# A hybrid decoder step on one core: both token groups through the trunk together, or one after the other in plain fp32

## The chip, the cores and the metric

The kernel runs on one core of one Trainium2 chip. A core has a matrix engine (TensorE, called PE in the profile; PEld is its loading of weights), a vector engine (VectorE, DVE), an activation engine (ScalarE, ACT), a general engine (GpSimd, POOL), a sequencer for transfers (SyncE, SP) and 16 DMA engines that all queues share. The metric is device time of one execution in microseconds (us); lower is better. A bank is one of the eight accumulators of TensorE, of 512 fp32 numbers per partition.

## What is computed

Two groups of tokens share every parameter: a prompt of 512 tokens and a sample batch of 8 sequences by 4 tokens. Everything is fp32.

```python
xn = rmsnorm(x, g_mix)                                # D_MODEL = 2048
xr, yr, ca, cb, ga, gb = split(xn @ w_in)             # 1024, 1024, 1024, 1024, 2048, 2048 columns
xc = causal_dwconv(xr, width 4)
h  = rglru(xc)                                        # gates from 8 heads of 128x128, linear recurrence over time
branch_a = (h * gelu(yr)) @ w_a
dc = causal_dwconv(ca * sigmoid(cb), width 31)
branch_b = silu(layernorm(dc)) @ w_b
x  = x + (sigmoid(ga) * branch_a + sigmoid(gb) * branch_b) @ w_out
q  = rmsnorm(x, g_ffn) @ w_q                          # 8 heads of 2 x 128
s1, s2 = q1 @ keys1.T, q2 @ keys2.T                   # 128 keys each
e, sv = top-16 of the 256 sums of top16(s1), top16(s2)    # 16 of 16384 experts, per token and head
x  = x + sum_k softmax(sv)_k * gelu(u_tab[e_k] . xn) * v_tab[e_k]
y  = rmsnorm(x, g_final)
```

The convolution and recurrence states are inputs and outputs too. The expert step reads 128 rows of u_tab and 128 of v_tab (8 KB each) for every tile of 128 tokens, per head and per k.

## The kernel before

The tokens stand in five tiles of 128. **Group A** is one prompt tile and the 32 sample tokens (160 columns wide), **group B** the other three prompt tiles (384 columns). T = 544 is both.

- **Start.** Tokens are loaded, normalised and turned by TensorE into channels by tokens, 16 steps of five transposes (L1522, L1523), then split for the next loop into a rounded part `xh` and a rest `xl` (L738 on ACT, L1098 on DVE).
- **Channel loop**, 8 chunks of 128 channels, both groups at once (`product3`, L1571 to L1573). Each chunk makes four products (xr, yr, ca, cb) over 16 k-steps. The operands are split, so a k-step is three reduced-precision terms (hi*hi, hi*lo, lo*hi) on two halves of 272 columns: 6 matmuls. ACT (L713) and DVE (L1188, three pairs of pieces per chunk) or POOL (L615) split the weights. Beside it DVE runs the short convolution (L1142, L1145), the recurrence (L1154 to L1171) and the 31-tap convolution (`long_conv`, L1199 to L1213).
- **Branch pairs** of group A, then its output projection, its norm, its query projection (`product_pair`, L1588, plain fp32: 96 matmuls per branch pair, 32 per step of output or query), with transposes back to tokens (L1706) and scores (L1715).
- The same of **group B**. In all this time DVE also does **group A's expert rows**: 160 key rows (`dot_row`, L1357: multiply a gathered u row by the token and add up) and 96 of the 160 value rows (`value_row`, L1366), with the routing (`route`, L1311 to L1344) of each unit of 16 rows.
- **Group B's rows**: 256 key rows (L1418) on DVE with 16 routings, beside group A's last 64 value rows on TensorE (L1766, a diagonal matrix times the row) and the building of dense expert weights (L1442, L1788).
- **Last**: v_tab is streamed whole through TensorE for two of B's tiles (L1818), while the third tile has 128 key rows and 128 value rows of its own on DVE. The change does not touch this part.

Orders are written by hand: each engine executes its list in order and waits on semaphores. On DVE and ACT the numbers p of A's 160 steps are dealt out by `STEPS_Q`, `steps_branch`, `steps_out`, `STEPS_NORM`, `steps_query`: 14 beside A's query, 84 beside B's eight branch pairs, 20 beside its output, 3 beside its norm, 39 beside its query. `VALUE_AT` says after which key row a value row comes. POOL issues the gathers (L607): a key row may be fetched three ahead (`SLOTS_U`), a value row two ahead (`SLOTS_V`), so the gather of value row v waits until row v-2 has been added. Weights come by SP in pieces of 512 KB into four buffers; each is reused as soon as it has been multiplied. In the channel loop a piece is 128 columns wide (`piece`, packets of 512 bytes), elsewhere 256 (`columns`, 1 KB). All scores of group B are written to DRAM (L1036) before its second unit can be routed, since the routing reads them back (L934).

## Time and profile before

| what | us |
|---|---|
| median of three runs (3850.53 to 3858.8) | 3855.13 |
| the profiled execution | 3870.63 |
| its span, first to last instruction | 3868.8 |
| joint channel loop | 57.0 to 461.9 |
| group A's branches, output, query | 461.9 to 917.5 |
| group B's branch pairs | 917.5 to 1435.5 |
| its output and query | 1435.5 to 1857.7 |
| end of A's expert rows | 1905.6 |
| B's 256 key rows | 1912.4 to 2793.7 |

TensorE is busy 79% of the span, VectorE 67%, ACT 15%, POOL 36%; the transfers move 1244.91 MB at 322 GB/s on average. Read the shares by stage: before 460 the DMA engines are a third busy and TensorE is full; from 917 on they are nearly full, and VectorE is at seven to nine tenths. A plain fp32 matmul leaves two records in the trace, a reduced-precision one leaves one.

### The profile page before, as it was taken

The page shows a single profiled execution, that of the slowest core. Times are in us where ns is not written, and L with a number is a line of the kernel's source. Part 1 is how long each engine was busy: PE and PEld are TensorE (multiplying, and loading weights), DVE is VectorE, ACT ScalarE, POOL GpSimd, SP SyncE. Part 2 cuts the span into 40 slices and gives each one's busy share as a digit, 9 for nine tenths or more (in the row PEclk, how much of TensorE's full clock was granted, in tenths as well). Part 3 has the DMA queues.
Part 4 walks back from the last instruction along what each step waited for, and adds up shares of the span by engine and source line. Part 5 has one row for each costly group of instructions (what it writes and reads, how often), then busy time and mean ns, then how long its engine had stood idle before and what let it go on. Part 6 is the DMA issues. An engine that isn't in the chain of part 4 may idle for free.

```text
span 3868.8 us, 34526 instructions
## 1 busy us (share of the span) xinstructions
PE 3051.7 (79%) x11870; PEld 1937.8 (50%) x11870; DVE 2591.0 (67%) x3611; ACT 586.0 (15%) x1115; POOL 1394.5 (36%) x876
## 2 busy tenths in 40 slices
PE   6999989987999989888345544544179899999993
PEld 6999989975555545555112212222143334444441
DVE  2788830035777766666688887889985556665658
ACT  4444320010010000111100001222250000000000
POOL 2000000003343333324476667666612234434344
PEclk9999999989999999999676677777599999999996
DMA  4222367759899998889899999999849999999998
GB/s 125 85 84 85 97 188 241 238 191 353 327 383 391 369 380 333 321 339 355 339 410 405 407 401 404 357 383 378 316 182 350 365 408 418 421 421 421 421 422 357
DMA packets 394596, 1244.91 MB, mean 322 GB/s; under 512 B 22785, under 2 KB 268289, under 8 KB 268959
## 3 DMA queue, kind: packets, MB, share of 16 engines
q0 software_dynamic: 120720, 876.60, 56.4%
q1 hardware_dynamic: 258944, 356.03, 26.4%
q10 hardware_dynamic: 14815, 10.87, 0.9%
q8 instruction: 56, 0.92, 0.1%
q14 instruction: 61, 0.50, 0.0%
HBM read 1232.26 MB, written 12.00 MB: 322 GB/s over the span
## 4 chain that ended last, share of the span: by engine, by line
DMA 35%; PE 27%; DVE 20%; issue 10%; POOL 5%; ACT 1%; SPq 1%; DVEq 0%; POOLq 0%; ACTq 0%
DMA region<-in_v_tab_dram,region 26%; PE ps L1588 14%; DVE region L1418 6%; DMA region<-in_u_tab_dram,region 5%; POOL region L607 5%; DVE region L1366 4%; PE ps L1571 3%; PE ps L1573 3%; PE ps L1572 3%; DVE region L1357 1%; DMA region<-in_w_q_dram 1%; DMA region<-scores_kept 1%; DVE region L1315 1%; DVE region L1312 1%; DMA region<-in_w_in_dram 1%
## 5 line engine op out<-in xcount | busy, mean ns | idle before, releaser
L607 POOL DMA_INDIRECT region<-in_u_tab_dram,region x544 | 886.8, 1630 | 1488.5 <-DVE region L1357 578.8
L1588 PE MATMUL ps<-region,region 128*128 128x160 f32 (+1 forms) x5120 | 1208.7, 399 | 67.3 <-DMA region<-in_w_out_dram 20.1
L1588 PEld LDWEIGHTS ps<-region,region 128*128 128x128 f32 x5120 | 852.2, 194 | 415.5 <-issue 43.1
L1418 DVE SCALAR_TENSOR_TENSOR region<-region,region 128x2048 f32<-128x2048 f32 x384 | 869.5, 2287 | 105.0 <-DMA region<-in_u_tab_dram,region 104.3
L1818 PE MATMUL ps<-region,region 128*128 128x512 f32 x2048 | 890.4, 597 | 38.8 <-DMA region<-in_v_tab_dram 38.0
L1366 DVE SCALAR_TENSOR_TENSOR region<-region,region,region 128x2048 f32<-128x2048 f32 x224 | 526.8, 2352 | 560.5 <-DMA region<-in_v_tab_dram,region 548.9
L1818 PEld LDWEIGHTS ps<-region,region 128*128 128x128 f32 x2048 | 389.7, 191 | 538.9 <-issue 483.2
L607 POOL DMA_INDIRECT region<-in_v_tab_dram,region x288 | 469.5, 1630 | 423.8 <-DVE region L1366 338.6
L1766 PE MATMUL ps<-region,region 128*128 128x512 f32 x512 | 355.8, 861 | 330.3 <-DMA region<-in_v_tab_dram,region 305.7
L1766 PEld LDWEIGHTS ps<-region,region 128*128 128x128 f32 x512 | 139.2, 285 | 532.2 <-issue 505.9
L1357 DVE SCALAR_TENSOR_TENSOR region<-region,region 128x2048 f32<-128x2048 f32 x160 | 363.0, 2286 | 17.7 <-DMA region<-in_u_tab_dram,region 17.6
L1571 PE MATMUL ps<-region,region 128*128 128x272 f32 x1024 | 297.4, 290 | 0.0
L1573 PE MATMUL ps<-region,region 128*128 128x272 f32 x1024 | 296.4, 289 | 0.0
L1572 PE MATMUL ps<-region,region 128*128 128x272 f32 x1024 | 294.8, 288 | 0.0
L1788 PE MATMUL ps<-region,region 128*128 128x128 f32 x512 | 90.0, 336 | 198.5 <-DVE region L1442 179.8
L1572 PEld LDWEIGHTS ps<-region,region 128*128 128x128 f32 x1024 | 193.1, 189 | 0.0
L1571 PEld LDWEIGHTS ps<-region,region 128*128 128x128 f32 x1024 | 192.7, 188 | 0.0
L1573 PEld LDWEIGHTS ps<-region,region 128*128 128x128 f32 x1024 | 192.6, 188 | 0.0
L1788 PEld LDWEIGHTS ps<-region,region 128*128 128x128 f32 x512 | 80.5, 240 | 220.8 <-issue 215.6
L945 ACT ACTIVATE region<-region 128x16 f32<-128x16 f32 x34 | 7.4, 217 | 1212.8 <-DVE region L1418 916.1
L1205 DVE SCALAR_TENSOR_TENSOR region<-region,region,region 128x512 f32<-128x512 f32 (+1 forms) x232 | 156.8, 747 | 0.0
L625 POOL DMA_DIRECT2D region<-in_x_prompt_dram x1 | 0.6, 576 | 388.5 <-DVE region L1260 388.5
(227 smaller groups left out, 1681.0 us busy)
## 6 DMA issues: line engine op xcount, KB each, us to landing
region<-in_v_tab_dram SPq DMA_DIRECT2D x128, 1024.0 KB
region<-in_w_in_dram SPq DMA_DIRECT2D x192, 512.0 KB
region<-in_w_out_dram SPq DMA_DIRECT2D x64, 512.0 KB
region<-in_w_q_dram SPq DMA_DIRECT2D x64, 512.0 KB
region<-in_w_a_dram SPq DMA_DIRECT2D x32, 512.0 KB
region<-in_w_b_dram SPq DMA_DIRECT2D x32, 512.0 KB
region<-in_u_tab_dram,region POOLq DMA_INDIRECT x544, 12.0
region<-in_x_prompt_dram SPq DMA_DIRECT2D x7, 1024.0 KB, 16.1
```

The costliest lines, as they stand in the source:

```text
L607: pool.indirect_dma_start(out=slot, out_offset=None, in_=rows_ap, in_offset=bass.IndirectOffsetOnAxis(ap=idx[:, k:k + 1], axis=0)).then_in ...
L1205: mark(stt(out=run, in0=glupad[:, k:k + TP], scalar=tap(k), in1=run, op0=ALU.mult, op1=ALU.add))
L1357: stt(out=u_a[s], in0=u_a[s], scalar=1.0, in1=xn_tile(u), op0=ALU.mult, op1=ALU.mult, accum_out=dots[u % 2][:, p % TOPK:p % TOPK + 1]).the ...
L1366: stt(out=total, in0=v_a[s], scalar=w_all[:, e:e + 1], in1=total, op0=ALU.mult, op1=ALU.add).then_inc(v_added, 1)
L1418: stt(out=u_b[s], in0=u_b[s], scalar=1.0, in1=xn_tile(UNITS_A + u), op0=ALU.mult, op1=ALU.mult, accum_out=dots[u % 2][:, k:k + 1]).then_in ...
L1571: mm(halves[j][:, a, :], hi, xh[:, k, h], start=(k == 0), stop=False)
L1572: mm(halves[j][:, a, :], hi, xl[:, k, h], start=False, stop=False)
L1573: last = mm(halves[j][:, a, :], lo, xh[:, k, h], start=False, stop=(k == DC - 1))
L1588: last = mm(outs[n][:, 0:WIDTH[g]], wide[s][:, q, n * P:(n + 1) * P], rhs(k), start=(k == 0), stop=(k == n_k - 1))
L1766: last = mm(acc[0][:, b * 512:(b + 1) * 512], diag[:, m % ND, :], v_a[n % SLOTS_V][:, b * 512:(b + 1) * 512], start=first, stop=last_row)
L1788: last = mm(bank(4 + n % 4)[:, q * P:(q + 1) * P], one_b[n % 2][:, q, :], one_a[n % 2][:, q, :], start=True, stop=True)
L1818: last = mm(acc[n][:, b * 512:(b + 1) * 512], w, v_t[s][:, b * 512:(b + 1) * 512], start=(c == 0), stop=False)
```

## The change

The two groups go through the trunk one after the other, A first, each with its own channel loop, branches, output and query.

- The loop products are plain fp32 like all others (`product`: one matmul of 160 or 384 columns per k-step); the splitting of tokens and weights (`product3`, `high`, `low`, `xh`, `xl`) is gone. The part of w_in that the channel loop reads, 32 MB, is loaded twice.
- The start loads and turns A's two tiles only; B's tokens are turned (`first_channels(1)`) inside A's branches.
- The convolutions and the recurrence are called once per group and chunk, with 128 (plus sample) or 384 columns. B's read their left context from A's end, kept in `ex`.
- A's 160 expert steps are dealt out anew: 14 beside A's query as before, 48 beside B's channel loop, 64 beside its branch pairs, 17 beside output, 2 beside norm, 15 beside query.
- Value rows of A: 128 (was 96) on DVE among these steps, 32 (was 64) on TensorE among B's key rows; one addition of the accumulator instead of two.
- Prompt tile 0 is now in group A (it was tile 3), and the state rows go out in two halves from B's branches.

```diff
-ROWS_W = 6 * TOPK
+ROWS_W = 8 * TOPK
...
-GROUP_P = 2 * TOPK
...
+USE_C = (0, USES_CC + USES_G)
+USE_G = (USES_CC, 2 * USES_CC + USES_G)
...
-def steps_branch(m):
-    return 14 + 21 * m // 2, 14 + 21 * (m + 1) // 2
+STEPS_1, STEPS_2, STEPS_3, STEPS_4 = 14, 62, 126, 143
+STEPS_NORM = (STEPS_4, STEPS_4 + 2)
+
+
+def steps_chunk(c):
+    return STEPS_1 + (STEPS_2 - STEPS_1) * c // CC, STEPS_1 + (STEPS_2 - STEPS_1) * (c + 1) // CC
+
+
+def steps_branch(i):
+    return STEPS_2 + (STEPS_3 - STEPS_2) * i // PAIRS, STEPS_2 + (STEPS_3 - STEPS_2) * (i + 1) // PAIRS
 
 def steps_out(j):
-    return 98 + 2 * min(j, 10), 98 + 2 * min(j + 1, 10)
+    return STEPS_3 + (STEPS_4 - STEPS_3) * j // DC, STEPS_3 + (STEPS_4 - STEPS_3) * (j + 1) // DC
 
 def steps_query(h):
-    return 121 + 39 * h // HEADS, 121 + 39 * (h + 1) // HEADS
+    first = STEPS_NORM[1]
+    return first + (ROWS_A - first) * h // HEADS, first + (ROWS_A - first) * (h + 1) // HEADS
...
-            with sp.Fori(0, CC) as c:
-                block_of(0, w_in_v, c * P, (half_used[0], c * 2 + 1), (ca_done, c + 1))
-                block_of(1, w_in_v, c * P + CH, (half_used[1], c * 2 + 1), (cb_done, c + 1))
-                sp.wait_ge(igate_done, c + 1)
+            def block_of(pair, w, col, frees0, frees1):
+
+                piece(PAIR[pair][0], w, 0, col, *frees0)
+                piece(PAIR[pair][1], w, 1, col, *frees1)
+
+
+            def chunk_first(g, c, freed=((), (), (), ())):
+                half, done = c * 2 + (2 * CC * g + 1), c + (CC * g + 1)
+                block_of(0, w_in_v, c * P, ((half_used[0], half), *freed[0]), ((ca_done, done), *freed[1]))
+                block_of(1, w_in_v, c * P + CH, ((half_used[1], half), *freed[2]), ((cb_done, done), *freed[3]))
+
+            def chunk_rest(g, c):
+                half, done = c * 2 + (2 * CC * g + 2), c + (CC * g + 2)
+                sp.wait_ge(igate_done, c + (CC * g + 1))
                 sp.dma_start(gw[:, 0, :], w_r_v[:, c, :]).then_inc(gw_landed, 16)
                 sp.dma_start(gw[:, 1, :], w_i_v[:, c, :]).then_inc(gw_landed, 16)
-                block_of(0, w_in_v, c * P + 2 * CH, (half_used[0], c * 2 + 2), (xr_done, c + 2))
-                block_of(1, w_in_v, c * P + 3 * CH, (half_used[1], c * 2 + 2), (yr_done, c + 2))
-            sp.wait_ge(ca_done, CC + 1)
-            sp.wait_ge(cb_done, CC + 1)
+                block_of(0, w_in_v, c * P + 2 * CH, ((half_used[0], half),), ((xr_done, done),))
+                block_of(1, w_in_v, c * P + 3 * CH, ((half_used[1], half),), ((yr_done, done),))
+
+            def chunk_weights(g, between, freed=((), (), (), ())):
+                chunk_first(g, 0, freed)
+                between()
+                chunk_rest(g, 0)
+                with sp.Fori(1, CC) as c:
+                    chunk_first(g, c)
+                    chunk_rest(g, c)
...
-            def low(slots, n):
-                for s in slots:
-                    pool.wait_ge(hi_ready[s], n + 1)
-                    nc.gpsimd.tensor_tensor(wlo[s], wraw[s], whi_f[s], ALU.subtract).then_inc(lo_ready[s], 1)
...
+            chunk_first(0)
+            chunk_rest(0)
+            for c in range(1, CC):
+                first, end = steps_chunk(c - 1)
+                mid = (first + end) // 2
+                expert_steps(first, mid)
+                chunk_first(c)
+                expert_steps(mid, end)
+                chunk_rest(c)
...
-            def low(pair, use):
-
-                for s in PAIR[pair]:
-                    dve.wait_ge(hi_ready[s], use + 1)
-                    tt(wlo[s], wraw[s], whi_f[s], ALU.subtract).then_inc(lo_ready[s], 1)
...
+                for j in range(2, CW):
+                    run = odd if j % 2 else even
                     step.before(2)
-                    mark(stt(out=run, in0=glupad[:, k:k + TP], scalar=tap(k), in1=run, op0=ALU.mult, op1=ALU.add))
-                    if k == 2:
+                    mark(stt(out=run, in0=k.glu[:, j:j + m], scalar=tap(j), in1=run, op0=ALU.mult, op1=ALU.add))
...
+            short_conv(1, 0)
+            recurrence_and_unit(1, 0)
+            for c in range(1, CC):
+                first, end = steps_chunk(c - 1)
+                mid = (first + end) // 2
+                expert_steps(first, mid)
+                short_conv(1, c)
+                long_conv(1, c - 1)
+                expert_steps(mid, end)
+                recurrence_and_unit(1, c)
+            long_conv(1, CC - 1)
+            expert_steps(*steps_chunk(CC - 1))
+            norm_center(1)
+            norm_scale(1)
...
-            def add_group(n):
-                dve.wait_ge(v_used, (GROUP_P, ROWS_P)[n])
-                dve.wait_ge(v_added, ROWS_W)
-                tt(xf[n], xf[n], acc[0], ALU.add).then_inc(acc_read, 1)
+            def add_group():
+                dve.wait_ge(v_used, ROWS_P)
+                tt(xf[1], xf[1], acc[0], ALU.add).then_inc(acc_read, 1)
...
+            def first_channels(g):
+                pe.wait_ge(xn_ready, TILES[g].stop)
+                back = 4 - g
                 for k in range(DC):
-                    if k >= 4:
-                        pe.wait_ge(xT_dve, k - 3)
-                    if k == 2:
-                        pe.wait_ge(staged_read, 1)
-                    for t in range(NT - 1):
-                        tr(ps[:, k % 4, t * P:(t + 1) * P], xt[:, t, k * P:(k + 1) * P], ident)
-                    tr(ps[:, k % 4, TP:T], xt[0:TS, NT - 1, k * P:(k + 1) * P],
-                       ident[0:TS, 0:TS]).then_inc(xT_done, 1)
-                pe.wait_ge(xT_act, DC)
-                pe.wait_ge(xT_dve, DC)
+                    if k >= back:
+                        pe.wait_ge(xT_dve if (k - back) % 2 else xT_act, CC * g + (k - back) // 2 + 1)
+                    out = first_bank(g, k)
+                    for n, t in enumerate(range(TILES[g].start, TILES[g].stop)):
+                        q = TS if t == 1 else P
+                        last = tr(out[:, n * P:n * P + q], xtn[t][0:q, k * P:(k + 1) * P], ident[0:q, 0:q])
+                    last.then_inc(xT_done, 1)
...
-            def product3(j, pair, n, ready=None):
+            pe.wait_ge(staged_read, 3)
+
+            def product(out, pair, use, g):
                 for half, s in enumerate(PAIR[pair]):
-                    pe.wait_ge(lo_ready[s], n + 1)
+                    pe.wait_ge(w_landed[s], use * 16 + 16)
                     for q in range(KP):
                         k = half * KP + q
-                        if ready is not None:
-                            pe.wait_ge(ready, k + 1)
-                        hi, lo = whi[s][:, q * P:(q + 1) * P], wlo[s][:, q * P:(q + 1) * P]
-                        for a in range(2):
-                            h = slice(a * TH, (a + 1) * TH)
-                            mm(halves[j][:, a, :], hi, xh[:, k, h], start=(k == 0), stop=False)
-                            mm(halves[j][:, a, :], hi, xl[:, k, h], start=False, stop=False)
-                            last = mm(halves[j][:, a, :], lo, xh[:, k, h], start=False, stop=(k == DC - 1))
+                        last = mm(out[:, 0:WIDTH[g]], wraw[s][:, q * P:(q + 1) * P], xp[g][:, k, :],
+                                  start=(k == 0), stop=(k == DC - 1))
...
+            def chunk_products(g):
+                k, m, n0 = chunk[g], PROMPT[g], CC * g
+                with pe.Fori(0, CC) as c:
+                    pe.wait_ge(xr_padded, c + (n0 + 1))
+                    product(bank(0), 0, c * 2 + USE_C[g], g).then_inc(xr_done, 1)
+                    pe.wait_ge(yg_ready, c + (n0 + 1))
+                    product(bank(2), 1, c * 2 + USE_C[g], g).then_inc(yr_done, 1)
+                    pe.wait_ge(staged_read, 5)
+                    pe.wait_ge(glu_ready, c + (n0 + 1))
+                    product(bank(6), 0, c * 2 + (USE_C[g] + 1), g).then_inc(ca_done, 1)
+
+                    pe.wait_ge(gw_landed, c * 32 + (32 * n0 + 32))
+                    pe.wait_ge(xcv_ready, c + (n0 + 2))
+                    for s, (read, done) in enumerate(((rg_ready, rgate_done), (ig_ready, igate_done))):
+                        pe.wait_ge(read, c + (n0 + 1))
+                        last = mm(bank(1 + 2 * s)[:, 0:m], gw[:, s, :], k.xcv[:, 0:m], start=True, stop=True)
+                        if g == 0:
+                            last = mm(bs(bank(1 + 2 * s)[:, m:NA]), gw[:, s, :], xc_s, start=True, stop=True)
+                        last.then_inc(done, 1)
+                    pe.wait_ge(cg_ready, c + (n0 + 1))
+                    product(bank(7), 1, c * 2 + (USE_C[g] + 1), g).then_inc(cb_done, 1)
...
+            def branches(g):
+                done = CC * (g + 1)
+                pe.wait_ge(xr_padded, done + 1)
+                gate_a(g, 0)
+                pe.wait_ge(rg_ready, done + 1)
+                gate_b(g, 0)
+                pe.wait_ge(glu_ready, done + 1)
+                pe.wait_ge(dc_ready, done)
+                if g:
+                    for c in range(CC):
+                        last = tr(ps[0:E_N, 3, c * P:(c + 1) * P], ex[:, c, :], ident)
+                    last.then_inc(exT_done, 1)
+                pe.wait_ge(ig_ready, done + 1)
+                norm_mean(g)
+                pe.wait_ge(ha_ready, done + 1)
+                if g:
+                    pe.wait_ge(exT_read, 2)
+                    branch_a(g, 0)
+                pe.wait_ge(mean_read, g + 1)
+                norm_squares(g)
+                if g == 0:
+                    first_channels(1)
+                    branch_a(g, 0)
+                pe.wait_ge(sd_ready, g + 1)
+                branch_b(g, 0, ready=lambda k: (silu_ready, g * CC + k + 1))
+                with pe.Fori(1, PAIRS) as i:
+                    branch_pair(g, i)
+
+            branches(0)
...
             second_half(0)
-            pe.wait_ge(xp_ready, 5)
-            with pe.Fori(0, DC // 2) as i:
-                branch_pair(1, i)
+            chunk_products(1)
+            branches(1)
             second_half(1)
```

On TensorE, the first chunk of the channel loop. Before (region_49 and region_50 are the two parts of the tokens, region_51 and region_52 those of the weights):

```order
L1563 ISA
L1571 MATMUL ps<-region_49,region_52 128x272
L1572 MATMUL ps<-region_50,region_52 128x272
L1573 MATMUL ps<-region_49,region_51 128x272
L1571 MATMUL ps<-region_49,region_52 128x272
```

With the change, in A's loop (region_62 is A's tokens, 49 to 52 the four weight buffers as they land):

```order
L1599 MATMUL ps<-region_62,region_49 128x160 x8
L1599 MATMUL ps<-region_62,region_50 128x160 x8
L1599 MATMUL ps<-region_62,region_51 128x160 x8
L1599 MATMUL ps<-region_62,region_52 128x160 x8
L1596 ISA
L1599 MATMUL ps<-region_62,region_49 128x160 x8
```

Six matmuls of 272 columns per k-step became one of 160 here, and one of 384 later in B's loop.

On VectorE, inside the 31-tap convolution. Before, the splitting of weights (L1188) stands between taps:

```order
L1205 SCALAR_TENSOR_TENSOR region_114<-region_59,region_116,region_114 128x512
L1188 TENSOR_TENSOR region_51<-region_55,region_52 128x1024
L1188 TENSOR_TENSOR region_51<-region_56,region_52 128x1024
L169 REGISTER_ALU
L1205 ISA
L1205 SCALAR_TENSOR_TENSOR region_61<-region_59,region_116,region_61 128x512
```

With the change, the end of the convolution in B's loop; region_78 to region_80 hold gathered key rows, region_81 a value row:

```order
L1239 SCALAR_TENSOR_TENSOR region_68<-region_121,region_123,region_68 128x384
L1246 TENSOR_TENSOR region_68<-region_68,region_121 128x384
L1376 SCALAR_TENSOR_TENSOR region_80,region_116<-region_80,region_54 128x2048
L1368 RECIPROCAL region_116<-region_116 128x1
L1370 SCALAR_TENSOR_TENSOR region_123<-region_116 128x16
L1376 SCALAR_TENSOR_TENSOR region_78,region_116<-region_78,region_54 128x2048
L1385 SCALAR_TENSOR_TENSOR region_53<-region_81,region_123,region_53 128x2048
```

Expert rows now stand between the convolution and the recurrence of every chunk of B.

On POOL, the gathers among B's key rows. Before:

```order
L607 DMA region_78<-in_v_tab_dram,region_116 128x2048
L607 DMA region_90<-in_u_tab_dram,region_116 128x2048
L607 DMA region_82<-in_u_tab_dram,region_116 128x2048
L607 DMA region_83<-in_u_tab_dram,region_116 128x2048
L607 DMA region_79<-in_v_tab_dram,region_116 128x2048
```

With the change:

```order
L635 DMA region_92<-in_u_tab_dram,region_123 128x2048
L635 DMA region_93<-in_u_tab_dram,region_123 128x2048
L635 DMA region_82<-in_v_tab_dram,region_123 128x2048
L635 DMA region_85<-in_u_tab_dram,region_123 128x2048
L635 DMA region_86<-in_u_tab_dram,region_123 128x2048
L635 DMA region_94<-in_u_tab_dram,region_123 128x2048
L635 DMA region_87<-in_u_tab_dram,region_123 128x2048
```

A value row came every three or four key rows; it comes every seven now.

## Rows read from the trace of the kernel before

**Rows 1.** The page, the span in 40 slices of 96.7 us, busy tenths

```profile
DVE  2788830035777766666688887889985556665658
```

**Rows 2.** Timeline of PE: start us, us, line, count [idle before <-releaser]

```profile
23.50 1.25 PE L1511 MATMUL ps<-region,region 76*128 76x76 f32 x8 [23.50 <-DMA region<-in_state_rnn_h_dram]
...
51.08 3.44 PE L1550 MATMUL ps<-region,region 120*128 120x120 f32 x16 [1.67 <-ACT region L738]
...
56.98 0.37 PE L1571 MATMUL ps<-region,region 128*128 128x272 f32 x1
...
466.81 20.57 PE L1588 MATMUL ps<-region,region 128*128 128x160 f32 x128 [4.89 <-DVE region L1230]
...
917.47 34.12 PE L1588 MATMUL ps<-region,region 128*128 128x384 f32 x96 [4.19 <-DVE region L1305]
```

**Rows 3.** The chain that ended last, in time: start us, us, what, records

```profile
566.28 165.17 PE ps L1588 x1216
...
835.85 13.47 DMA region<-in_w_q_dram
...
1607.99 20.64 PE ps L1588 x64
```

**Rows 4.** Busy time by stretch: PE, PEld, DVE, ACT, POOL, clock, DMA share, GB/s

```profile
200.00:250.00 50.00, 50.00 (x390) 49.04 (x389) 41.66 (x68) 20.82 (x27) 0.00 (x0) 1.00 0.30 87
...
2000.00:2100.00 100.00, 48.66 (x64) 18.76 (x64) 82.97 (x129) 8.99 (x19) 67.61 (x39) 0.68 1.01 413
```

**Rows 5.** Timeline of DVE: scan, short and long convolution of one chunk

```profile
209.75 1.31 DVE L1166 TENSOR_TENSOR_SCAN region<-region 128x552 f32<-128x552 f32 x1
...
223.37 2.72 DVE L1145 SCALAR_TENSOR_TENSOR region<-region,region,region 128x568 f32<-128x568 f32 x3 [0.15 <-DVE region L1142]
...
240.22 8.70 DVE L1205 SCALAR_TENSOR_TENSOR region<-region,region,region 128x512 f32 x13
```

**Rows 6.** Timeline of DVE: the same operation at 160 and at 384 columns

```profile
495.23 1.98 DVE L1238 TENSOR_TENSOR region<-region,region 128x160 f32<-128x160 f32 x8
...
534.78 3.84 DVE L1238 TENSOR_TENSOR region<-region,region 128x384 f32<-128x384 f32 x8
```

**Rows 7.** Timeline of DVE: key rows (L1357) and a value row (L1366)

```profile
1115.76 2.29 DVE L1357 SCALAR_TENSOR_TENSOR region<-region,region 128x2048 f32<-128x2048 f32 x1
...
1117.97 2.29 DVE L1357 SCALAR_TENSOR_TENSOR region<-region,region 128x2048 f32<-128x2048 f32 x1
...
1124.11 2.35 DVE L1366 SCALAR_TENSOR_TENSOR region<-region,region,region 128x2048 f32<-128x2048 f32 x1 [3.84 <-DMA region<-in_v_tab_dram,region]
1126.38 2.28 DVE L1357 SCALAR_TENSOR_TENSOR region<-region,region 128x2048 f32<-128x2048 f32 x1
```

**Rows 8.** Timeline of POOL: the gather that this value row waited for

```profile
1114.11 2.54 POOL L607 DMA_INDIRECT region<-in_v_tab_dram,region  x1 [0.30 <-issue]
```

**Rows 9.** Timeline of PE: the waits in group B's output and query

```profile
1455.65 43.29 PE L1588 MATMUL ps<-region,region 128*128 128x384 f32 x128 [20.12 <-DMA region<-in_w_out_dram]
...
1655.83 7.78 PE L1538 MATMUL ps<-region,region 128*128 128x128 f32 x48 [25.15 <-DVE region L1290]
...
1807.23 2.93 PE L1715 MATMUL ps<-region,region 128*128 128x128 f32 x12 [12.43 <-ACT region L878]
```

**Rows 10.** Timeline of ACT: scores of B to DRAM, then the wait for A's last row

```profile
1857.68 0.52 ACTq L1036 DMA_DIRECT2D scores_kept<-region  x1
...
1905.59 0.22 ACT L945 ACTIVATE region<-region 128x16 f32<-128x16 f32 x1 [46.02 <-DVE region L1357]
```

**Rows 11.** Timeline of DVE: first and last operation of one routing, and the sixteenth routing's last

```profile
1925.16 0.29 DVE L1311 MAX8 region<-region 128x8 f32<-128x128 f32 x1
...
1935.00 0.18 DVE L1344 SCALAR_TENSOR_TENSOR region<-region 128x16 int32<-128x16 f32 x1
...
2759.28 0.17 DVE L1344 SCALAR_TENSOR_TENSOR region<-region 128x16 int32<-128x16 f32 x1
```

**Rows 12.** Who waited for whom from 1912 to 2740: us, times, longest

```profile
DVE region L1418 <- DMA region<-in_u_tab_dram,region: 89.1, 79, 6.9
```

744 lines of the change are left out of this document (345 added, 399 removed).

## The prediction

> **What bounds the kernel now.** I read the slices first: VectorE climbs from the fifth slice on and stays at seven to nine tenths from the middle to the end [rows 1]. The reader should not stop at that average. The edges of the stages come from the timeline of PE [rows 2], and each stage has its own limit.
>
> In the joint channel loop PE never pauses and the transfers need a third of the DMA engines (first of [rows 4]). From the first product at 56.98 to 466.81 - 4.89 = 461.92 it makes 8 x 4 x 16 x 6 = 3072 matmuls, 0.132 us each. Group A's branches are PE too, at 165.17 / 1216 = 0.136 us a record, so 0.272 us for a plain fp32 matmul of 160 columns; at 384 columns it is 2 x 20.64 / 64 = 0.645 us [rows 3]. B's eight pairs took 1435.5 - 917.5 = 518 us where 8 x 96 x 0.645 = 495 are due: PE with a few waits for weights. B's rows (1912 to 2794) are bound by transfers and VectorE together: the DMA share is 1.01 at 413 GB/s with DVE 83% busy (second of [rows 4]), and 89 us of DVE's idle time wait for a gathered key row [rows 12]. What is moved out of DMA's way there is worth time; what is moved into the loops of B costs DVE time that the joint loop did not have.
>
> **The change part by part.** All terms are against the profiled execution, 3870.6 us.
>
> *Start.* The parameter rows, for which PE waits, land at 23.5, and the channels are turned until 51.08; then 6 us of other transposes follow [rows 2]. Two transposes per step instead of five need about 10 us, from 24.8 on; with the 6 us the first product starts near 41. **-16.**
>
> *A's channel loop.* PE: 64 x 0.272 + 4 gate matmuls of at most 0.272 = 18.5 us a chunk. DVE's share comes from slopes: the same operation takes 1.98 / 8 = 0.248 us at 160 columns and 3.84 / 8 = 0.480 at 384, so 1.04 ns a column [rows 6]; a tap of the long convolution takes 8.70 / 13 = 0.669 us at 512 [rows 5], so 0.27 at 128 and 0.536 at 384. A chunk of A is then 29 x 0.27 + 3 (the sample windows, openings, closing) + 2 (short) + 4 (recurrence) = 17 us: hidden, barely. Weights: the joint loop's 0.30 share lasted 50.6 us a chunk; the same bytes in 18.5 us are a share of 0.82, hidden. 8 x 18.5 = 148 against 404.9: **-257.** Up to 1.5 us more a chunk if DVE's and ACT's chain shows.
>
> *A's branches, output, query.* Gone: the 4.9 us wait at the entry [rows 2], the statistics of B's norm, the tail of a 512-wide convolution. New: 48 transposes of B's tokens with their copies, about 11 us, since three banks must be read back. Net **-8** (between -20 and +5).
>
> *B's channel loop.* This is the large term. PE: 64 x 0.645 + 2 x 0.645 = 42.6 us a chunk. DVE: convolution 29 x 0.536 + 1.4 = 16.9; short convolution: 2.72 / 3 = 0.907 a tap at 568 [rows 5], 0.716 at 384, three of them and 0.9 around them = 3.0; recurrence: seven operations near 0.5 and a scan of 1.0 (1.31 at 552) = 4.7. Sum 24.6. Beside these stand steps 14 to 61: 48 key rows at 1117.97 - 1115.76 = 2.21 us, 40 value rows at 1126.38 - 1124.11 = 2.27 [rows 7], three routings at 1935.0 - 1925.2 + 0.2 = 10 [rows 11]: 106 + 91 + 30 + 2 = 229, or 28.6 a chunk. Both are on one engine and nothing overlaps them: 53.2. Then the gathers: a value row's gather was issued at 1114.11 and used at 1124.11, 10 us [rows 7, 8], and it may be issued only two value rows ahead. Each half chunk has three key rows and 2.5 value rows; two of them are fetched beforehand, the third was issued 6.6 us before its turn, so 0 to 3.4 us are waited per half. I take 3.8 a chunk: **57 us**, so DVE sets the pace and PE idles 14. Seven such chunks are 399; the first has no steps and costs PE's 42.6, its recurrence 5 and 2 for weights, 50. **+449**, with 53 to 61 a chunk, +421 to +477.
>
> *B's first pairs.* After the last recurrence DVE still has the convolution (17) and six steps with values (31) before it centres the norm. Centring, squares, root, reciprocal and scaling are a chain through three engines of about 13 us, and the matmuls of branch b end 10 later: 71 us in. Then ten rows and a routing lie ahead of the first merge (60 us), for which PE's third product of pair 1 waits: pair 1 is done 146 us in. Six pairs at 61.9 and 5 of waits for weights: 522 against 518. **+4.** The steps (8 a pair, about 50 us with their waits) then stay under PE's 61.9.
>
> *Output and query of B.* 34 steps where 62 stood. The 20.1 us for w_out stay, since the same three loads stand before it; the 25.2 us of DVE before the transposes lose a step (-5); the 12.4 us in which ACT was held up by steps go (-12); some waits of DVE (-3) [rows 9]. **-20** (-10 to -30).
>
> *Hand-over.* B's last score leaves at 1857.7, but A's last row came at 1905.6, 46 us of waiting [rows 10]; the first routing from DRAM began at 1925.2, 67 us after [rows 11]. Now the rows are done in time, and the routing waits for the 3 MB of scores to be written and read back beside ten gathers of 1 MB: 13 MB at 413 GB/s are 31 us, plus the read back, so about 37. **-30** (-20 to -45).
>
> *B's key rows.* 32 gathers fewer. At 413 GB/s one takes 2.54 us, 81 in all; DVE's own need is 16 x 2.21 + 10 + 0.6 = 46 us a unit (50 with the dense building) against 54.9 measured between first and sixteenth routing [rows 11]. Neither limit gives all, as they take turns: **-65** with the addition that is dropped (bounds -15 and -90, the latter what DVE waits [rows 12]).
>
> The part after 2794 is untouched. **Sum:** -16 - 257 - 8 + 449 + 4 - 20 - 30 - 65 = **+57**, 3928 by the profiled execution. That one is 15.5 above the median of 3855.1, so I forecast **3912**.
>
> In short, PE's plain fp32 needs 0.272 + 0.645 = 0.917 us a k-step where six reduced terms needed 0.79, so the loops alone lose 60 us of PE; and the overlap that was to pay for it is bounded by DVE.
>
> *A rule on short vector operations.* The taps above carry 0.131 us beyond their columns (0.669 less 512 x 1.04 ns). The Trainium skill, "VectorE: DVE Perf Modes", section "The TRN2 errata", gives 58 cycles plus one per column for SBUF operations at 0.96 GHz. By that a tap of 384 would take 0.46 us and B's eight convolutions 17 us less; the sum would be +40. The measured taps decide.
>
> **The rivals.**
>
> *1. Weights starve in B's loop (slower still).* The loop's pieces go in 512-byte packets, twice as many as elsewhere, beside gathers of 8 KB rows. With 1 KB packets and gathers in flight, PE waited for a piece that took 13.5 us [rows 3]. Four buffers cover three pieces of 8 x 0.645 = 5.2 us, 15.5 us. If a 512-byte piece takes 23 us beside gathers, PE gets one every 23 / 15.5 x 5.2 = 7.7 us, 62 a chunk with the gates, and where it coincides with DVE's waits about 67: 7 x 10 = +70, **3982**. For: the packets. Against: only 28 of 57 us of a chunk have gathers queued, and PE has 14 us to spare. It decides from about 20 us a piece.
> The Trainium skill, "DMA: Bandwidth & Descriptors", section "Queues, rings and completion order", says that a DMA engine takes turns between its queues packet by packet. By that rule small weight packets lose their turn to row gathers, and this rival's 3982 would be the time; no loop of the kernel before shows 512-byte pieces beside gathers.
>
> *2. The steps hide in B's loop (faster).* Place: DVE in chunks 1 to 7. If steps and convolution together fit under PE's 42.6, the loop is 7 x 14.4 = 101 shorter: **3811**. It turns into a gain below 49 us a chunk. Against: 24.6 + 28.6 are both engine time of one engine from measured durations. For: only shorter taps, or gaps in my durations that are pitch and not work.
>
> *3. The relief among B's rows does not come.* DVE is at 83% there; if rows arrive late for latency and not for bandwidth, 32 gathers fewer give 15 and not 65: **3962**.
>
> **How the numbers follow.** Forecast, DVE-paced loop, 3865 to 3955: 0.60. Rival 1: 0.16. Rival 2: 0.13. Rival 3: 0.11. The range runs from 3840 to 3985: it takes in the chunk at 53 to 61 (-28, +28), the bounds of the hand-over and of B's rows, rival 3 and half of rival 1; it leaves out half of rival 1 and nearly all of rival 2, 0.19. This kernel can be told from no change at about 0.2%, 7.7 us. Faster than 3847: 0.15 (rival 2 and a lucky tail of the forecast). Within: 0.07. Slower: 0.78.
>
> **What would show it.** PE's first product near 41, A's loop done near 190, B's starting near 640. In B's loop a period of 57 us with PE busy about three quarters and waiting for DVE (its gate matmuls after the short convolution, and ca after the unit); if it waits for w_in it is rival 1, if PE is full it is rival 2. B's last score near 2015, first routing from DRAM some 37 us later, and a routing period near 50 us. The forecast is wrong if a tap at 384 is far from 0.54 us, if a step costs other than 4.8 us plus waits, or if A's loop shows waits between the chunks.

## The result

The changed kernel takes 3989.74 us (median of 4 runs, 3984.06 to 3998.99), the kernel before 3856.97 us in the same comparison: a ratio of 1.0348, 95% interval 1.0321 to 1.0375. It is 133 us slower where 57 were forecast, and lies 5 us outside the range. The profiled execution has a span of 3991.5 us, 122.7 more than that of before.

The slices of the changed kernel, span in 40 parts of 99.8 us, answer [rows 1]: VectorE is at eight and nine tenths already in the eighth to eleventh slice, B's channel loop, and has a hole in the 21st, the wait ahead of B's key rows.

```profile
DVE  3820034998877755446528898999986566656658
```

Timeline of PE in the changed kernel, against [rows 2], [rows 9] and [rows 10] (columns as there):

```profile
30.90 1.25 PE L1543 MATMUL ps<-region,region 76*128 76x76 f32 x8 [30.90 <-DMA region<-in_state_rnn_h_dram]
...
48.35 13.21 PE L1599 MATMUL ps<-region,region 128*128 128x160 f32 x96
...
201.02 17.55 PE L1615 MATMUL ps<-region,region 128*128 128x160 f32 x128
...
638.42 34.22 PE L1599 MATMUL ps<-region,region 128*128 128x384 f32 x96 [4.17 <-DVE region L1324]
...
932.02 2.93 PE L1636 MATMUL ps<-region,region 128*128 128x384 f32 x4 [5.76 <-DVE region L1168]
...
1067.07 41.44 PE L1615 MATMUL ps<-region,region 128*128 128x384 f32 x128
...
1141.20 8.50 PE L1694 MATMUL ps<-region,region 128*128 128x384 f32 x16 [16.33 <-ACT region L823]
...
1229.99 33.69 PE L1615 MATMUL ps<-region,region 128*128 128x384 f32 x96 [13.74 <-DVE region L1278]
...
1664.08 43.70 PE L1615 MATMUL ps<-region,region 128*128 128x384 f32 x128 [7.08 <-DMA region<-in_w_out_dram]
...
1875.74 2.83 PE L1570 MATMUL ps<-region,region 128*128 128x128 f32 x12 [35.56 <-DVE region L1309]
...
1889.64 41.52 PE L1615 MATMUL ps<-region,region 128*128 128x384 f32 x128 [0.69 <-ACT region L903]
...
2074.39 1.60 PE L1740 MATMUL ps<-region,region 128*128 128x128 f32 x12 [0.96 <-ACT region L877]
```

Read from the top: first product 48, A's loop done 201, B's loop 638 to 1067 (its last recurrence ends at 1089.5), pairs to 1657 (1664.08 less the wait of 7), output, norm, query, last score 2076. Timeline of VectorE in the changed kernel: a tap of the long convolution at 384 columns (two, for the pitch), A's last key row, B's next key row, the first routing from DRAM with its first and last operation, the last operation of the sixteenth:

```profile
932.60 0.61 DVE L1239 SCALAR_TENSOR_TENSOR region<-region,region,region 128x384 f32<-128x384 f32 x1
933.13 0.61 DVE L1239 SCALAR_TENSOR_TENSOR region<-region,region 128x384 f32<-128x384 f32 x1
...
2013.60 2.28 DVE L1376 SCALAR_TENSOR_TENSOR region<-region,region 128x2048 f32<-128x2048 f32 x1
...
2076.20 2.29 DVE L1451 SCALAR_TENSOR_TENSOR region<-region,region 128x2048 f32<-128x2048 f32 x1 [60.31 <-PE ps L1740]
...
2101.63 0.30 DVE L1330 MAX8 region<-region 128x8 f32<-128x128 f32 x1 [10.19 <-DMA region<-scores_kept]
...
2111.47 0.17 DVE L1363 SCALAR_TENSOR_TENSOR region<-region 128x16 int32<-128x16 f32 x1
...
2882.53 0.17 DVE L1363 SCALAR_TENSOR_TENSOR region<-region 128x16 int32<-128x16 f32 x1
```

The stages side by side, each term as the prediction cut it (span against span):

| term | forecast | measured | from |
|---|---|---|---|
| start | -16 | -8.7 | 48.3 against 57.0 |
| A's channel loop | -257 | -252 | 152.7 against 404.9 |
| A's branches, output, query | -8 | -18 | 437.4 against 455.6 |
| B's channel loop to its last recurrence | +449 | +451 | 638.4 to 1089.5 |
| B's pairs | +4 | **+49.5** | 567.5 against 518 |
| B's output, norm, query | -20 | -2.6 | 419.6 against 422.2 |
| last score to the first routing's end | -30 | -42 | 34.9 against 77.3 |
| sixteen routings | -65 | -53 | 771.1 against 824.3 |
| sum (after it -0.5) | +57 | +123 | |

The large terms, the two loops, came within 5 us. One term, the pairs, carries 45 of the 66 us that are missing in the span, and output, norm and query another 17; the others nearly cancel.

### The profile page after: what moved, and what is told of

Read it like the earlier page. It is cut to its first block, busy times and chain, and to the rows that moved or that the text cites. A ratio compares the mean times of both kernels' runs of the same rounds, so it can differ in the third digit from the quotient of the medians.

```text
span 3991.5 us, 32152 instructions
## 1 busy us (share of the span) xinstructions
PE 2991.4 (75%) x10622; PEld 1830.8 (46%) x10622; DVE 2631.0 (66%) x3962; ACT 558.0 (14%) x1105; POOL 1428.3 (36%) x862
## 4 chain that ended last, share of the span: by engine, by line
DMA 32%; PE 30%; DVE 23%; issue 8%; POOL 3%; ACT 2%; SPq 1%; ACTq 0%; DVEq 0%; POOLq 0%
PE ps L1615 23%; DMA region<-in_v_tab_dram,region 20%; DVE region L1451 8%; PE ps L1599 5%; DMA region<-in_u_tab_dram,region 4%; DVE region L1385 3%; POOL region L635 3%; DVE region L1239 3%; DMA region<-in_w_in_dram 2%; DMA region<-in_w_q_dram 2%; DMA region<-in_w_a_dram 1%; DVE region L1376 1%; DMA region<-scores_kept 1%; DVE region L1475 1%; DVE region L1334 1%
## 5 line engine op out<-in xcount | busy, mean ns | idle before, releaser
L1615 PE MATMUL ps<-region,region 128*128 128x160 f32 (+1 forms) x5120 | 1211.4, 399 | 78.7 <-DMA region<-in_w_q_dram 22.2
L1615 PEld LDWEIGHTS ps<-region,region 128*128 128x128 f32 x5120 | 847.9, 194 | 433.5 <-issue 47.4
L1385 DVE SCALAR_TENSOR_TENSOR region<-region,region,region 128x2048 f32<-128x2048 f32 x256 | 601.7, 2350 | 487.3 <-DMA region<-in_v_tab_dram,region 475.5
L1840 PE MATMUL ps<-region,region 128*128 128x512 f32 x2048 | 885.3, 593 | 31.0 <-DMA region<-in_v_tab_dram 30.1
L635 POOL DMA_INDIRECT region<-in_v_tab_dram,region x288 | 524.2, 1820 | 633.4 <-DVE region L1385 576.3
L1840 PEld LDWEIGHTS ps<-region,region 128*128 128x128 f32 x2048 | 387.2, 190 | 528.4 <-issue 477.0
L1599 PE MATMUL ps<-region,region 128*128 128x160 f32 (+1 forms) x2048 | 491.7, 403 | 31.9 <-DVE region L1216 27.5
L1788 PE MATMUL ps<-region,region 128*128 128x512 f32 x256 | 182.1, 877 | 326.9 <-DMA region<-in_v_tab_dram,region 318.6
L1599 PEld LDWEIGHTS ps<-region,region 128*128 128x128 f32 x2048 | 343.6, 195 | 178.5 <-issue 51.3
L1376 DVE SCALAR_TENSOR_TENSOR region<-region,region 128x2048 f32<-128x2048 f32 x160 | 364.5, 2284 | 13.7 <-DMA region<-in_u_tab_dram,region 11.1
L1788 PEld LDWEIGHTS ps<-region,region 128*128 128x128 f32 x256 | 71.9, 296 | 428.8 <-issue 423.0
L1810 PEld LDWEIGHTS ps<-region,region 128*128 128x128 f32 x512 | 86.8, 258 | 283.6 <-issue 278.7
L1239 DVE SCALAR_TENSOR_TENSOR region<-region,region,region 128x128 f32<-128x128 f32 (+1 forms) x240 | 114.4, 477 | 0.0
L1278 DVE TENSOR_TENSOR region<-ps,region 128x160 f32<-128x160 f32 (+1 forms) x32 | 13.9, 435 | 149.8 <-PE ps L1615 149.8
L1330 DVE MAX8 region<-region 128x8 f32<-128x128 f32 (+1 forms) x102 | 34.4, 337 | 110.4 <-ACT region L929 87.0
L1239 DVE SCALAR_TENSOR_TENSOR region<-region,region 128x128 f32<-128x128 f32 (+1 forms) x224 | 106.7, 476 | 0.0
L1475 DVE TENSOR_SCALAR region<-region 128x128 f32<-128x128 f32 x256 | 70.6, 348 | 4.6 <-PE ps L1810 4.5
```

The costliest lines, as they stand in the source:

```text
L635: pool.indirect_dma_start(out=slot, out_offset=None, in_=rows_ap, in_offset=bass.IndirectOffsetOnAxis(ap=idx[:, k:k + 1], axis=0)).then_in ...
L1239: mark(stt(out=run, in0=k.glu[:, j:j + m], scalar=tap(j), in1=run, op0=ALU.mult, op1=ALU.add))
L1376: stt(out=u_a[s], in0=u_a[s], scalar=1.0, in1=xn_tile(u), op0=ALU.mult, op1=ALU.mult, accum_out=dots[u % 2][:, p % TOPK:p % TOPK + 1]).the ...
L1385: stt(out=total, in0=v_a[s], scalar=w_all[:, e:e + 1], in1=total, op0=ALU.mult, op1=ALU.add).then_inc(v_added, 1)
L1475: last = ts_(one_a[n % 2][:, q, :], count, turned[:, 0, col:col + 1], turned[:, 2, col:col + 1], ALU.is_equal, ALU.mult)
L1599: last = mm(out[:, 0:WIDTH[g]], wraw[s][:, q * P:(q + 1) * P], xp[g][:, k, :], start=(k == 0), stop=(k == DC - 1))
```

## The experiments

Each time is given as its ratio to the kernel before, measured on the same chip beside it; 0.01 is 38.6 us. The changed kernel stands at 1.0348 (1.0321 to 1.0375). The intervals of norm_first, act_mid6, value_ahead, throttle_ahead, rows_w_96, deal_before and throttle touch or overlap this one, so their differences of 1 to 21 us in the whole are at the edge of what can be told or below it; what they teach is read from the stages. "Six pairs" is the time from the end of B's second pair to the end of its eighth, for which 576 matmuls of 0.645 us make 371 us: 383 in the kernel before, 404 in the changed one. Of the 33 us above 371, 22.8 are waits for weights; much of the rest is slower matmuls right behind such a wait (16 records took 7.12 us behind a wait of 2.71, 5.43 in most other places).

### What sets the pace of B's channel loop

In the changed kernel's loop TensorE waits for VectorE and not for weights. Waits of PE from 681 to 1067 (what waited for what: us, times, longest):

```profile
PE ps L1636 <- DVE region L1168: 36.9, 6, 14.0
PE ps L1599 <- DVE region L1216: 27.5, 5, 10.8
PE ps L1599 <- DMA region<-in_w_in_dram: 0.3, 1, 0.3
```

**three_taps**

```diff
-                for j in range(2, CW):
+                for j in range(2, CW if g == 0 else 3):
```

> The changed kernel with 3 instead of 31 taps in B's long convolution (28 taps of each chunk are left out), all steps and gathers as they were. Theory (VectorE's own sum sets the pace): 28 x 0.53 = 14.8 us a chunk less on VectorE, period 57 to 43, seven chunks -95, and the last convolution -15: near 3885. Rival (gathers share the transfers with the loop's weights, and this makes the period): VectorE only waits longer for its rows, the period stays above 50 us, 3950 or more.

Measured: 1.0091 (1.0063 to 1.0119), 99 us less than the changed kernel, and the loop's products end at 1001 instead of 1067. So VectorE's sum was the pace. The period is 45.7 us and not 42.6: now the weights, in packets of 512 bytes beside the same gathers, come late by 11.9 us in five places, with the DMA share at 0.97 (0.79 before the edit). That is rival 1 of the prediction, and it begins only where the loop is faster than it was.

**deal_before**, the steps as in the kernel before:

```diff
-STEPS_1, STEPS_2, STEPS_3, STEPS_4 = 14, 62, 126, 143
-STEPS_NORM = (STEPS_4, STEPS_4 + 2)
+STEPS_1, STEPS_2, STEPS_3, STEPS_4 = 14, 14, 98, 118
+STEPS_NORM = (STEPS_4, STEPS_4 + 3)
...
-    return STEPS_3 + (STEPS_4 - STEPS_3) * j // DC, STEPS_3 + (STEPS_4 - STEPS_3) * (j + 1) // DC
+    return 98 + 2 * min(j, 10), 98 + 2 * min(j + 1, 10)
```

> The changed kernel with A's 160 steps dealt as in the kernel before: 14 beside A's query, none beside B's channel loop, 84 beside its pairs, 20 output, 3 norm, 39 query. Theory (VectorE sets the pace of B's loop: 24.6 us of its own and 28.6 of steps a chunk): without steps the loop is TensorE's, about 43 us a chunk, its last recurrence near 985 instead of 1090 (-105); the six steps that stood between the last convolution and the norm are gone (-25 to -30 before the first merge); the 39 steps beside the query end some 45 us after the last score instead of before it, and the hand-over is 77 us again (+42). Sum near 3895. Rival (the loop's weights in 512-byte packets, or plain fp32 itself, make the loop slow): the period stays above 50 us a chunk, and the time above 3950.

Measured: 1.0379 (1.0354 to 1.0404), no faster than the changed kernel, where 95 us of gain were expected. The loop did what the theory said (42.6 us a chunk without a pause, products done at 982.5, 85 us earlier). More than that was given back: pairs 627 us instead of 589, 19 more from there to the last score, and 88 us instead of 35 from the last score to the end of the first routing. The deal that cost 518 us of pairs in the kernel before costs 627 here, and so pointed to the wrong term. Stretch, its length, busy time of the engines, clock, DMA share and GB/s of its six pairs:

```profile
1154.00:1610.00 456.00, 400.15 (x1163) 226.91 (x1162) 348.50 (x380) 32.41 (x55) 205.15 (x130) 0.95 0.99 384
```

The six pairs take 453 us here and move 173.4 MB; in the kernel before they take 383 us and move 145.9 MB. The rates, 384 and 381 GB/s, are nearly the same, with a DMA share of 0.99 and 1.00: in this run the longer stretch goes with the larger sum of bytes.

### What makes B's pairs long

Waits in the changed kernel from 1067 to 1656:

```profile
DVE region L1385 <- DMA region<-in_v_tab_dram,region: 98.6, 43, 8.3
...
PE ps L1615 <- DMA region<-in_w_in_dram: 17.2, 12, 2.7
PE ps L1694 <- ACT region L823: 16.3, 1, 16.3
PE ps L1615 <- DVE region L1278: 13.7, 1, 13.7
...
PE ps L1615 <- DMA region<-in_w_a_dram: 6.6, 3, 2.9
...
PE ps L1615 <- ACT region L833: 5.0, 1, 5.0
...
PE ps L1615 <- DMA region<-in_w_b_dram: 3.4, 3, 1.5
```

35 us are the norm and the first merge behind VectorE's steps, 27 us are weights.

**norm_first**: the last chunk's six steps go into the pairs, 8 or 9 a pair (on ScalarE alike).

```diff
             long_conv(1, CC - 1)
-            expert_steps(*steps_chunk(CC - 1))
             norm_center(1)
```

> The changed kernel with the six steps of the last chunk moved from ahead of B's norm into the eight pairs (8 or 9 a pair instead of 8). Theory (31 us of steps between the last convolution and the norm hold TensorE, which waits 16.3, 5.0 and 13.7 us in the first two pairs): 20 to 30 us less, near 3965; the pairs after the second are as they were. Rival (TensorE waits for weights in the pairs whatever the order, and six steps more there add gathers and waits): no gain, 3980 to 3995.

Measured: 1.0294 (1.0267 to 1.0322), 21 us less. The second pair ends at 1223 instead of 1253, the six pairs take 410 instead of 404. Both theories hold in part: the norm was late by its place in VectorE's list, and more steps beside the pairs cost TensorE more waits.

**value_transfers_small**: 126 of the 128 gathers of value rows are left out, each replaced by a transfer of 64 KB.

```diff
                 s = V_SLOTS[n][0]
-                gather(v_rows, v_a[s], va_landed[s], idx_all, e)
+                if SLOTS_V <= n < ROWS_W:
+                    part(pool)
+                    pool.dma_start(v_a[s][:, 0:P], v_rows[0:P, 0:P]).then_inc(va_landed[s], 16)
+                else:
+                    gather(v_rows, v_a[s], va_landed[s], idx_all, e)
```

> The changed kernel with 126 of the 128 gathers of value rows (1 MB each) replaced by a transfer of 64 KB into the same buffer with the same semaphore; key rows, VectorE's work and all orders as they were (the sample tile and tile 0 are then computed from stale rows). Theory (bursts of gathers take the DMA engines from the weights of B's pairs; the six pairs from 1250 on take 406 us where 371 are due): the waits for weights go, pairs -30; B's loop loses VectorE's waits for value rows, 2 to 4 us a chunk, -20; near 3935. Rival (the waits for weights come from how the pieces are freed and issued, not from the gathers): pairs as they were, only the -20 of the loop, 3970.

Measured: 1.0065 (1.0045 to 1.0086), 109 us less, twice what was expected. The six pairs take 371 us without one wait, the wait for w_out is gone, the loop ends 27 us earlier (6 of them lie ahead of it). So the gathers of value rows are what delays the weights; whether by their bytes or by the way they come, this run does not say.

**rows_w_96**: 96 value rows on VectorE and 64 on TensorE, with the two additions of the kernel before.

```diff
-ROWS_W = 8 * TOPK
+ROWS_W = 6 * TOPK
```

> The changed kernel with 96 value rows on VectorE and 64 on TensorE, as in the kernel before (two additions of the accumulator), deal of the steps unchanged. New theory (the 32 value rows that went to VectorE put gathers of 1 MB ahead of the last score, where they compete with the weights of B's pairs): the six pairs from the third on lose half of the 33 us that they are above 371, -15; B's loop has 10 value rows and their waits less, -30; the routing period among B's key rows goes back from 51.4 to 55 us, +53. Sum near 3990, no difference, but with a last score 45 to 60 us earlier. Rival (the period of B's key rows fell for another reason, the free half of the pool's queue or the later start): period stays near 51.4 and the time falls to 3940.

Measured: 1.0328 (1.0306 to 1.0349). As forecast, the parts cancel: last score at 2022.5 instead of 2076, routing period 55.0 us instead of 51.4. The six pairs fell to 376.5, by more than I said; the loop did not become faster at all.

**before_rows_w_128**: the same one part, the other way round, in the kernel before.

```diff
-ROWS_W = 6 * TOPK
+ROWS_W = 8 * TOPK
```

> The kernel before with that one part of the change alone: 128 value rows on VectorE, 32 on TensorE, one addition. Theory (gathers against weights in B's pairs): 84 steps with 72 value rows instead of about 54 beside eight pairs are 20 MB of gathers and 6 MB of weights a pair, more than the 61.9 us of products hide; pairs 518 to about 590, A's last row 60 to 90 us later, against it -53 among B's key rows: 3880 to 3910. Rival (value rows on VectorE are a gain by themselves, and the pairs are slow in the changed kernel for its order): pairs stay within 10 us of 518, time 3800 to 3840.

Measured: 1.0101 (1.0071 to 1.0130), 39 us more. B's pairs take 591 us instead of 518, with 61 us of waits for weights instead of 8; the last score is 80 us later; the routing period falls to 51.4. So value rows moved ahead of the last score lengthen the pairs without any part of the new trunk. But this run is not the changed kernel in small. It moves 220.6 MB beside its pairs where the kernel before moves 190.2, at nearly the same rate (373 and 367 GB/s): at 413 GB/s, the rate among B's key rows, the 30 MB more are 74 us, by this estimate all of the 73. The changed kernel has fewer steps there: its six pairs have 96 gathers and 141.5 MB where the kernel before has 102 and 145.9, and a DMA share of 0.91 instead of 1.00, and are 21 us longer all the same. Its loss is not the sum of the bytes.

### The sum of the bytes, or how many gathers are in flight

**act_mid6**: ScalarE stages the next unit's scores before it waits for gate products.

```diff
-                mid = min(first + 4, end)
+                mid = min(first + 6, end)
```

> The changed kernel with one number changed on ScalarE: in each of B's pairs it does six steps' work ahead of the gate sigmoids, not four, so that the scores of the next unit are staged before it waits for TensorE (VectorE waited 53.7 us in three routings for that between 1250 and 1657). Theory (gathers starve the weights because they come in bursts after such holds): VectorE's rows come evenly, TensorE's waits for weights in the six pairs fall from 33 to about 15, time near 3970. Rival (it is the sum of the gathers, not their bursts): the pairs take as long as before within 5 us, 3985 to 3995.

Measured: 1.0306 (1.0282 to 1.0329), 16 us less; the six pairs 394 instead of 404, waits for weights in them 15.7 instead of 22.8 us, and VectorE's three waits for staged scores (53.7 us) are gone. The same steps, spread more evenly (DMA share 0.97 instead of 0.91), cost less, but most of the waits stay.

**before_value_ahead, rows_w_96_value_ahead, value_ahead.** In the kernel before GpSimd issues a value gather behind the next key row's gather, which itself waits for a buffer. Timelines of POOL and DVE, kernel before: the key gather waited 5.24 us for VectorE, the value gather came after it, and its row was waited for:

```profile
1707.09 0.93 POOL L607 DMA_INDIRECT region<-in_u_tab_dram,region  x1 [5.24 <-DVE region L1357]
1708.33 0.95 POOL L607 DMA_INDIRECT region<-in_v_tab_dram,region  x1 [0.30 <-issue]
```

```profile
1719.52 2.35 DVE L1366 SCALAR_TENSOR_TENSOR region<-region,region,region 128x2048 f32<-128x2048 f32 x1 [3.10 <-DMA region<-in_v_tab_dram,region]
```

```diff
-                if p - 1 in VALUE_AT:
-                    v = VALUE_AT[p - 1]
+                if p in VALUE_AT:
+                    v = VALUE_AT[p]
```

> The kernel before with one edit on GpSimd: the gather of the value row that comes after key row p is issued behind the gather of key row p, not behind that of key row p+1 (which waits until key row p-2 is multiplied). Theory (VectorE's waits for value rows, 66.7 us in 21 rows beside B's query and 110 us beside its pairs, come from this place in the list, since a gather lands 9 to 10 us after its issue): the gather starts up to 4 us earlier and two thirds of those waits go; A's last row, now 48 us behind the last score, ends 30 us or more earlier, and the time falls to 3815 to 3835. Rival (the gathers are slow because the DMA engines are full): as many waits, and what VectorE gains comes back as waits of TensorE for weights; 3850 to 3870.

> The changed kernel with 96 value rows on VectorE and this edit of GpSimd's list. In the run with 96 rows, B's loop had 19 us less of VectorE's work in its last seven chunks than the changed kernel and 19 us more of its waits for value rows, and took the same time. Theory (the waits come from the place in the list): they fall from 46 to under 20 us there, the loop ends 25 to 30 us earlier, time near 3960. Rival (they come from the fullness of the DMA engines, the share is 0.74 there): the loop stays within 8 us.

> The changed kernel (128 value rows on VectorE) with the same edit. Here nearly every key row has a value row, and the buffer of value row v comes free (row v-2 added) just after the key row that releases the next key gather: by the theory of the list there is next to nothing to gain, 3980 to 3995, with waits for value rows within 10 us of those in the changed kernel. Rival (any earlier issue shortens the waits): a gain of 20 us or more, as in the two other kernels of this set.

Measured: before_value_ahead 1.0256 (1.0232 to 1.0280), 99 us **slower** than the kernel before. VectorE's waits for value rows beside the pairs did fall, from 110 to 20.5 us (38.6 us of waits for key rows are new), but the pairs grew from 518 to 621. Waits in that stretch:

```profile
PE ps L1588 <- DMA region<-in_w_in_dram: 54.4, 16, 5.2
PE ps L1588 <- DMA region<-in_w_a_dram: 24.0, 9, 5.4
...
PE ps L1588 <- DMA region<-in_w_b_dram: 3.8, 1, 3.8
```

and the DMA issues (KB each, median us from issue to landing) and the busy times, of this kernel and then of the kernel before:

```profile
region<-in_w_in_dram SPq DMA_DIRECT2D x60, 512.0 KB, 10.2
region<-in_w_a_dram SPq DMA_DIRECT2D x16, 512.0 KB, 25.0
```

```profile
917.00:1538.00 621.00, 538.31 (x1533) 307.05 (x1534) 388.20 (x452) 41.86 (x71) 299.84 (x145) 0.93 0.86 327
```

```profile
917.00:1435.00 518.00, 506.18 (x1535) 295.13 (x1536) 366.02 (x437) 41.51 (x70) 197.58 (x135) 0.98 0.97 367
```

The bytes are not quite the same: 145 gathers instead of 135 fall into the stretch, 203.3 MB instead of 190.2. At 413 GB/s these 13 MB are 32 us, an estimate; 71 of the 103 us are left, and in them the DMA share is lower and the weights are later. What changed is seen in the GB/s of 40 equal slices of the stretch, the kernel before and then this one:

```profile
GB/s 348 381 404 223 82 217 401 406 383 406 399 399 382 348 366 397 406 400 387 398 343 408 399 379 395 408 401 401 224 386 388 404 405 337 403 372 307 395 403 395
```

```profile
GB/s 312 399 394 112 367 412 412 410 358 294 306 400 407 412 151 175 399 230 101 248 412 405 412 406 376 143 399 412 412 291 101 324 352 101 240 412 399 412 411 376
```

Weights alone, 512 KB in 5.16 us, are 102 GB/s. Six slices lie below 160 GB/s instead of one, and eleven at 410 or more instead of none: the gathers now come in bursts with gaps between them, and TensorE waits 82 us for weights instead of 8. The trace of the kernel before has no landing times here, so that a piece lands later in a burst is inferred from these waits and from the 25.0 us of w_a. VectorE's waits were a brake that spread the gathers. The rival had named the waits that come back, but neither theory had them so much larger than the gain.

rows_w_96_value_ahead: 1.0389 (1.0362 to 1.0416). Its loop shows the gain that the list theory promised: products done at 1021 instead of 1067. Busy times of the last seven chunks, rows_w_96 and then this kernel:

```profile
681.00:1067.00 386.00, 322.70 (x934) 185.45 (x933) 325.71 (x533) 77.16 (x101) 103.33 (x65) 0.92 0.74 256
```

```profile
681.00:1021.00 340.00, 313.48 (x934) 181.49 (x933) 326.03 (x536) 77.22 (x101) 113.38 (x65) 0.95 0.84 291
```

VectorE works 326 us in both, and waited 46.3 us for value rows in the first, 0 in the second. The changed kernel itself has 344.7 us of work and 27.3 of these waits: a value row less on VectorE had only made the wait for the next one longer. But the six pairs rose from 376.5 to 446 us, and the whole is slower. value_ahead: 1.0301 (1.0279 to 1.0322), 18 us less than the changed kernel. There I had expected nothing. Its waits for value rows beside the pairs fell from 98.6 to 55.7 us, but this brought nothing there: the six pairs take 417.5 us instead of 404. The gain lies elsewhere: the loop's products are done 13 us earlier, at 1054, and the last score at 2062 instead of 2076. So the earlier gather lengthens the six pairs in all three kernels, by 82, 69 and 14 us.

**throttle**: for the 64 steps beside the pairs a key row is fetched two ahead instead of three.

```diff
-                        pool.wait_ge(dot_a, p - SLOTS_U + 1)
+                        pool.wait_ge(dot_a, p - SLOTS_U + (2 if STEPS_2 <= p < STEPS_3 else 1))
```

> The changed kernel with one wait on GpSimd tightened for the 64 steps beside B's pairs: a key row is fetched two ahead instead of three, so that at most four gathers are in flight, not five; everything else as it was. Theory (a piece of weights is late when it is queued beside too many gathers at once, not when the sum of the bytes is too large): TensorE's waits for weights in the pairs fall from 27 us to under 10 and the six pairs from 404 to about 380, VectorE's steps take longer but fit; near 3965. Rival (only fewer gathers help): the pairs stay at 67 us, or VectorE becomes their bound, 3990 to 4010.

Measured: 1.0403 (1.0373 to 1.0433), 21 us slower. DMA issues beside the pairs, the changed kernel and then throttle:

```profile
region<-in_w_in_dram SPq DMA_DIRECT2D x61, 512.0 KB, 12.4
```

```profile
region<-in_w_in_dram SPq DMA_DIRECT2D x61, 512.0 KB, 8.2
```

Waits beside the pairs in throttle; a wait for weights is not among them:

```profile
PE ps L1615 <- DVE region L1278: 63.5, 7, 39.9
PE ps L1694 <- ACT region L823: 19.7, 1, 19.7
...
DVE region L1385 <- DMA region<-in_v_tab_dram,region: 214.8, 47, 12.8
```

With at most one gather less in flight all 27 us of waits for weights are gone. But the value gather stands behind the delayed key gather, VectorE waits 215 us instead of 99, and the merges are late: the six pairs take 403 us as before, now at VectorE's pace. This run alone does not show the depth as the cause, since while TensorE waits for a merge the weights catch up, and since 90 gathers instead of 96 fall into its six pairs (132 MB instead of 141).

**throttle_ahead**: throttle, and the value gather behind its own row's key gather beside the pairs.

```diff
-                if p - 1 in VALUE_AT:
-                    v = VALUE_AT[p - 1]
+                for at in (p - 1, p):
+                    if at in VALUE_AT and at == (p if STEPS_2 <= at < STEPS_3 else p - 1):
+                        v = VALUE_AT[at]
```

> The changed kernel with both edits of GpSimd's list for the 64 steps beside B's pairs: key rows two ahead, and the value gather behind the key gather of its own row. In the run with the first edit alone TensorE waited 0 us for weights (27 before) and a piece landed in 8.2 us (12.4), but VectorE's waits for value rows rose from 99 to 215 us and TensorE waited 63 us for merges. Theory: the value gather stood behind the delayed key gather; with its own place the waits fall to about 110 us, eight steps take 55 us and hide under 61.9, and both gains stay: six pairs near 376, near 3965. Rival (four gathers in flight can't feed VectorE whatever the order): merges late again, above 4000.

Measured: 1.0314 (1.0282 to 1.0347). Waits for weights 19.5 us instead of 27.2, merges late once (16.1 us; 13.7 in the changed kernel), six pairs 394 instead of 404. VectorE's waits are the 110 us of the theory (57 for value rows, 53 for key rows), but 376 was too hopeful. The whole is better than throttle and no better than value_ahead (1.0301), whose loop is shorter. What the depth does is seen best between these two, which in the pairs differ only in the throttle. Stretch of the six pairs, value_ahead and then throttle_ahead:

```profile
1231.00:1648.00 417.00, 387.88 (x1152) 222.88 (x1150) 262.56 (x290) 27.33 (x47) 194.32 (x97) 0.97 0.90 342
```

```profile
1255.00:1650.00 395.00, 379.45 (x1153) 219.64 (x1152) 264.27 (x291) 27.34 (x47) 190.32 (x98) 0.99 0.95 361
```

The bytes are the same (142.6 and 142.4 MB, 97 and 98 gathers), VectorE's work too. With at most four gathers in flight instead of five the six pairs take 394 us instead of 417.5, and the waits for weights in them are 15.1 us instead of 29.0.

### Putting the parts together

**spread**: 21 steps beside the loop, 69 beside the pairs, 26, 2 and 28 behind them, norm first.

```diff
-STEPS_1, STEPS_2, STEPS_3, STEPS_4 = 14, 62, 126, 143
+STEPS_1, STEPS_2, STEPS_3, STEPS_4 = 14, 38, 104, 130
```

> The changed kernel with a deal made by the transfers' and VectorE's room: 21 steps beside B's loop (3 a chunk, 18 us of room), the norm ahead of any further step, 69 beside the pairs (8 or 9 each), 26 beside output, 2 norm, 28 query. Theory: the loop is TensorE's (-85 to -100), the norm comes without steps (-20), the pairs stay near 67 us each, output and query gain 5 to 15 us of waits, A's last row ends within 15 us of the last score: 3890 to 3915, still above the kernel before. Rival (what leaves the loop comes back as waits elsewhere, as with the deal of before): 3960 or more.

Measured: 1.0188 (1.0152 to 1.0223), 62 us less than the changed kernel. The loop's products end at 977.6 (-90) and the pairs take 570 us (-20), but 26 steps beside the output make VectorE late for the norm (71 us from the last transposes to the query, not 49), and the query takes 12 more.

**combined, combined_deal, combined_throttle, combined_throttle_ahead.** combined is norm_first with act_mid6 and the earlier value gather beside the loop. The second also deals 28, 66, 20, 2 and 30 steps (14, 46, 108, 128); the third adds the throttle beside the pairs; the fourth has the earlier value gather there too. In the first three and the fourth this line reads (STEPS_B is the first step beside the pairs):

```diff
-                    if at in VALUE_AT and at == (p if at < STEPS_B else p - 1):
+                    if at in VALUE_AT and at == (p if at < STEPS_3 else p - 1):
```

> The changed kernel with three edits that were measured apart: B's norm ahead of the last six steps, value gathers issued one key row earlier for the steps beside B's loop only, and six steps' work of ScalarE ahead of the gate sigmoids. If they add up: -20, -13, -13, near 3945. If they share a cause (VectorE's rows reach the pairs in bursts either way), 3955 to 3970.

> As combined, with 28 steps beside B's loop instead of 42, 66 beside its pairs, 20 output, 2 norm, 30 query. Theory: VectorE's 24.6 us and four steps of 4.8 us are about 45 us a chunk against TensorE's 42.6, so the loop ends 60 to 70 us earlier than in the changed kernel (near 1000); the pairs stay at 66 to 68 us; 10 to 20 us come back in output and query: 3890 to 3910. Rival (all that leaves the loop comes back): 3940.

> As combined_deal, with at most two key rows ahead beside the pairs. If the depth of the gathers is what delays the weights: the six pairs near 380 instead of about 400, 3870 to 3885, and no version of the two passes gets below the kernel before (3863), since its floor is TensorE's 60 us more in the loops. If not: within 5 us of combined_deal.

> As combined_throttle, with the value gather behind the key gather of its own row beside the pairs too. By the same theory TensorE's waits for merges (57 us) go and the weights stay in time: 25 to 35 us less than combined_deal, near 3900, still 35 to 40 above the kernel before. Rival: as combined_throttle, 3950.

Measured: 1.0244 (1.0214 to 1.0273), 1.0156 (1.0130 to 1.0183), 1.0219 (1.0192 to 1.0246), 1.0124 (1.0091 to 1.0156). The three edits of combined add up for the larger part (40 us of 50: 21 and 16 apart, and 13 in value_ahead's loop). The last has the lowest ratio of the two passes, though its interval overlaps that of combined_deal: 86 of the 133 us recovered, loop done at 987, pairs 564 us, last score at 1980, and still 48 us above the kernel before. The throttle without the earlier value gather is a loss here too. With it, the six pairs take 395 us instead of 424 in combined_deal, at the same bytes beside the pairs (190 MB); a version of combined_deal with the earlier gather and no throttle was not run.

**before_ahead_tail**: the kernel before, value gathers one key row earlier for key rows 150 to 159 only.

```diff
-                if p - 1 in VALUE_AT:
-                    v = VALUE_AT[p - 1]
+                for at in (p - 1, p):
+                    if at in VALUE_AT and at == (p if at >= 150 else p - 1):
+                        v = VALUE_AT[at]
```

> The kernel before with the value gathers one key row earlier for key rows 150 to 159 only, which run when no weights are left to load. There VectorE waits 18.7 us for value rows between the last score at 1857 and A's last row at 1906. Theory (bursts of gathers cost time only where weights are due): 10 to 15 us of these waits go and come off the time: 3850, a gain of 0.3 to 0.4%. Rival (an earlier gather only lands later when ten gathers are queued): no difference.

Measured: 0.9980 (0.9963 to 0.9997), a gain of 0.2% that the interval just separates from none. VectorE's waits from the last score to A's last row, the kernel before and then this one:

```profile
DVE region L1366 <- DMA region<-in_v_tab_dram,region: 18.7, 6, 7.0
```

```profile
...
DVE region L1358 <- DMA region<-in_u_tab_dram,region: 5.7, 7, 1.7
DVE region L1367 <- DMA region<-in_v_tab_dram,region: 4.7, 5, 1.9
```

Of 18.7 us for value rows 4.7 are left, 5.7 are new for key rows, and A's last row ends 39 us behind the last score instead of 48. The edit that cost 99 us beside the weights is a small gain where none are loaded. It is the only version that beats both kernels.

## Why the prediction was wrong

**Start.** -8.7 instead of -16: the parameter rows land at 30.9, not 23.5. The turning itself took the 10 us of the working.

**A's loop and A's part.** Right. From the third on a chunk takes 18.3 us (18.5 in the working); the first two cost 6 us more, 3.0 of them a wait for the short convolution. A's part gained 18 us where the bounds were -20 and +5.

**B's loop.** Right in size and in engine. A tap is 0.53 us (0.54 in the working; its own slope gives 0.53), the last recurrence ends at 1089.5 where the working from 638.4 gives 1087, and PE waited for VectorE at the two places named. In part two misses cancel: from one recurrence to the next it is 58.3 us (57 in the working), and the first chunk took 43 instead of 50. One thing in it was wrong and did not show: I had the steps as work plus some waits. The runs with 96 rows show that the waits are what is left of a gather's landing time, so less work would not have made the chunk shorter by as much. Rival 1 did not occur here (0.3 us); three_taps shows its start. That the measured 3990 lies near its 3982 is chance: its place was this loop. Rival 2 did not occur.

The Trainium skill, "VectorE: DVE Perf Modes", section "The TRN2 errata", with 58 cycles and one per column, makes 0.46 us of this tap. The trace has 0.53, so the fixed part is larger here, and the measurement decides.

**B's pairs: the step that failed.** "Six pairs at 61.9 and 5 of waits for weights" took the waits from the pairs of before, where 84 steps ran. It counted the steps (64 instead of 84) and so saw relief. The relief in gathers and bytes was there, if small (96 gathers instead of 102 in the six pairs), and it did not help: with 128 value rows instead of 96 a gather of 1 MB stands behind nearly every key row, and I did not ask how closely the gathers follow each other and how many of them are in flight at once. The six pairs took 404 us instead of 376, with 22.8 us of waits for weights instead of 5; 7 of these 28 us were there to be read, as the kernel before needed 383. This is the mechanism of rival 1, in a stage where I had put it at 5 us. value_transfers_small and rows_w_96 show that it is the gathers of value rows (371 us with nearly all of them left out, 376.5 with 96 of 128), value_ahead and throttle_ahead that the number in flight changes the weights' waits with the same bytes (29.0 to 15.1 us), act_mid6 that gaps and bursts cost as well (404 to 394 us). In before_rows_w_128 and deal_before the DMA engines are full (share 0.97 to 0.99) and the extra bytes account for the extra time, so these two show another limit and not the one that the changed kernel met. The Trainium skill, "DMA: Bandwidth & Descriptors", section "Queues, rings and completion order", says that a DMA engine takes turns between queues packet by packet. That weights in 1 KB packets land late beside 8 KB rows (medians of 8.2, 12.4 and 25.0 us, against 4.7 for w_in over the whole changed kernel) agrees with it; that they land later with more gathers in flight it does not say.

The first two pairs took 164 us where 146 were said. VectorE waited 29 us for value rows in them, before the norm and the first merge.

**Output and query.** -2.6 instead of -20. The wait for w_out fell to 7 us and ScalarE's hold of 12 us went, as said or better. But the norm came 16 us later, since VectorE still had steps and rows to add when the last transposes were done (35.6 us of wait instead of 25.2), and weights of the query were waited for.

**Hand-over and B's rows.** -42 and -53 against -30 and -65, both inside their bounds, together right. Rival 3 did not occur: the period is 51.4 us, and it returned to 55.0 when the 32 gathers returned.

**The base.** I took off 15.5 us, by which the profiled execution of before lay above its median. The profiled execution of the changed kernel lies 3.6 us above its own, so 10 to 12 us of the miss are this subtraction and no part of the kernel.

## What to carry to other kernels

When work with large gathers is moved beside streamed weights, first compare the bytes of each stage with the rate that the transfers reach when they are full (before_rows_w_128 lost its 73 us by this sum). Then ask how closely the gathers come and how many can be in flight at once, and compare a piece's landing time at that depth with what the buffers cover: the changed kernel lost 21 us in its six pairs with fewer bytes and a lower DMA share than before. A wait on an engine with slack can be a useful brake: before it is removed, ask what it holds back. And a term that is copied from the old trace holds only if everything that shares its resource is the same there.

## What was new about the hardware

A piece of 512 KB of weights in 1 KB packets landed in a median of 8.2 us with at most four gathers of 1 MB in flight, 12.4 us with at most five, and w_a's pieces in 25.0 us in before_value_ahead. Pairs that were longer by 103 us went with a DMA share that fell from 0.97 to 0.86. With the same 142 MB, at most four gathers in flight instead of five shortened six pairs from 417.5 to 394 us.

After a wait of 5.8 us for VectorE the four records of the gate matmuls took 2.93 us (the row of 932.02 above); without a wait they took 1.45 us. Timeline row of PE and busy times of the two stretches, changed kernel:

```profile
672.48 1.45 PE L1636 MATMUL ps<-region,region 128*128 128x384 f32 x4
```

```profile
932.00:935.00 3.00, 2.98 (x5) 1.77 (x6) 3.00 (x7) 0.59 (x2) 0.00 (x0) 0.50 1.02 407
935.00:960.00 25.00, 25.00 (x74) 14.48 (x74) 24.75 (x34) 4.25 (x5) 7.48 (x4) 0.94 0.58 202
670.00:715.00 45.00, 45.00 (x141) 26.51 (x140) 30.93 (x55) 11.21 (x15) 6.03 (x4) 1.00 0.59 196
```

The granted clock is 0.50 in the three microseconds after the wait, the lower of TensorE's two levels (1.2 GHz), and comes back to the upper one (2.4 GHz) behind them. So the four holds of 5.8 to 14.0 us ahead of the gate matmuls in B's loop cost TensorE their own length and 1.5 us more each, which no term of mine had; behind the two of 0.98 and 1.16 us the four records took 1.56 us.
